# Prompt weight blocks nine beats apart, compressed rows turned later, and GpSimd signalling the end of a ranking stage

## Time and profile before

| what | value |
|---|---|
| three runs | 2637.49 us median (2624.43 to 2644.32) |
| the profiled execution | 2624.34 us, span 2622.6 us |
| granted TensorE clock, mean of the span | 0.857 |
| busy share of the span | PE 75%, DVE 56%, POOL 53%, PEld 38%, ACT 28% |
| moved by DMA | 806.19 MB, mean 307 GB/s |
| packets of GpSimd's queue (the expert rows and cached pages) | 68.1% of the time of 16 engines |
| packets of SP's queue (weights, stored rows) | 14.1% |

### The profile page before, as it was taken

The page is one execution under the profiler, slowest core; times in us unless marked ns, Lnnn a source line. Parts: engine busy times, 40 slices in busy tenths (PEclk is TensorE's granted clock), DMA queues, the critical chain, the costliest instruction groups (busy, mean ns, idle before and its releaser), DMA issues. The chain is left out here.

```text
span 2622.6 us, 23237 instructions
## 1 busy us (share of the span) xinstructions
PE 1959.6 (75%) x7254; PEld 1008.9 (38%) x7254; DVE 1462.1 (56%) x3293; ACT 721.4 (28%) x1716; POOL 1389.9 (53%) x1415
## 2 busy tenths in 40 slices
PE   5979798688988767986857889676677777748346
PEld 4446467244444324545412345352122323227111
DVE  1024346576465623674954268666366777763864
ACT  1111112366675402431211135111132333310001
POOL 2021016667677734674774356658465555443774
PEclk9975699798999887897979889788898999965579
DMA  7141509887999998899889989997989999896797
GB/s 222 65 160 44 177 1 335 311 306 283 383 408 411 406 385 294 325 351 403 321 326 400 307 328 347 386 335 255 390 335 360 358 358 372 296 349 232 275 392 305
DMA packets 253891, 806.19 MB, mean 307 GB/s; under 512 B 41813, under 2 KB 46425, under 8 KB 244249
## 3 DMA queue, kind: packets, MB, share of 16 engines
q0 software_dynamic: 176496, 673.82, 68.1%
q1 hardware_dynamic: 77128, 130.89, 14.1%
q10 hardware_dynamic: 144, 0.00, 0.0%
HBM read 798.90 MB, written 14.04 MB: 310 GB/s over the span
## 5 line engine op out<-in xcount | busy, mean ns | idle before, releaser
L3142 PE MATMUL g_acc<-g_vrow,g_diag 128*128 128x512 f32 (+1 forms) x1432 | 766.3, 670 | 260.2 <-ACT g_diag L3120 128.5
L3013 POOL DMA_INDIRECT g_vrow<-in_peer_v_dram,f_idx x576 | 598.2, 1039 | 458.1 <-PE g_acc L3142 161.6
L2997 POOL DMA_INDIRECT f_u<-in_peer_u_dram,f_idx x576 | 579.1, 1005 | 375.3 <-DVE g_dot L3078 244.3
L3078 DVE CUSTOM_DVE_ANT_0 f_u<-f_u,g_h_ps 128x1024 f32<-128x1024 f32 x576 | 685.1, 1214 | 116.8 <-DMA f_u<-in_peer_u_dram,f_idx 66.2
L3142 PEld LDWEIGHTS g_acc<-g_vrow,g_diag 128*128 128x128 f32 (+1 forms) x1432 | 262.9, 198 | 659.4 <-issue 460.4
L3055 DVE SCALAR_TENSOR_TENSOR x<-g_vrow,g_w,x 128x1024 f32<-128x1024 f32 x218 | 280.6, 1287 | 22.1 <-DMA g_vrow<-in_peer_v_dram,f_idx 11.6
L1068 ACT ACTIVATE g_slab<-g_side 64x256 f32<-64x256 f32 x512 | 193.8, 378 | 116.9 <-PE g_side L1019 110.8
L3039 DVE TENSOR_TENSOR g_w<-g_gelu,f_gate 128x4 f32<-128x4 f32 x144 | 26.3, 183 | 357.3 <-ACT g_gelu L3110 356.8
L1030 PE MATMUL g_side<-g_slab 128*128 128x512 f32 x256 | 144.2, 646 | 50.1 <-ACT g_slab L1068 50.0
L3120 ACT ACTIVATE g_diag<-const,g_w 128x128 f32<-128x128 f32 (+1 forms) x358 | 126.0, 381 | 195.8 <-DVE g_w L3039 194.4
L1170 PE MATMUL g_side<-g_slab 128*128 128x512 f32 (+3 forms) x288 | 129.6, 593 | 60.2 <-DMA g_slab<-in_nsa_w_in_dram 60.2
(11 more groups left out here) (402 smaller groups left out, 2407.8 us busy)
## 6 DMA issues: line engine op xcount, KB each, us to landing
g_slab<-in_nsa_w_in_dram SPq DMA_DIRECT2D x15, 2048.0 KB, 18.9
g_slab<-in_peer_w_q_dram SPq DMA_DIRECT2D x14, 2048.0 KB, 19.8
mp_w<-in_mlstm_w_in_dram SPq DMA_DIRECT2D x6, 2048.0 KB, 10.6
g_slab<-in_nsa_w_out_dram SPq DMA_DIRECT2D x6, 2048.0 KB, 14.4
f_u<-in_peer_u_dram,f_idx POOLq DMA_INDIRECT x576, 7.5
g_vrow<-in_peer_v_dram,f_idx POOLq DMA_INDIRECT x576, 7.5
g_slab<-in_state_win_kv_dram SPq DMA_DIRECT2D x8, 1024.0 KB, 8.9
out_win_s_dram<-in_state_win_kv_dram SPq DMA_DIRECT2D x1, 8128.0 KB
```

The costliest lines, as they stand in the source:

```text
L2997: pool.indirect_dma_start(u[:, i % RU, :], None, u_table, bass.IndirectOffsetOnAxis(ap=idx[:, col:col + 1], axis=0), element_offset=layer ...
L3013: pool.indirect_dma_start(vrow[:, i % RV, :], None, v_table, bass.IndirectOffsetOnAxis(ap=idx[:, col:col + 1], axis=0), element_offset=lay ...
L3078: dve.tensor_tensor_reduce(row, row, h_ps[:], 1.0, 0.0, ALU.mult, ALU.add, dot[:, g % 2, k:k + 1]).then_inc(dotted, 1)
L3142: mm = pe.matmul(acc[0:n, a, :], diag[:, q % (2 * GRP), 0:n], vrow[:, i % RV, a * 512:a * 512 + 512], start=first and on_pe[i] == on_pe[GR ...
```

## The change

- `NP_AT` has a row for prompts and one for the decode work. In the prompt stages the jobs begin at beats 0, 9, 18, 27, 29 and 38 of the projection instead of 0, 6, 12, 18, 20 and 26; their lengths stay. Steps that stood at fixed beats behind the jobs (adding the gate's bias, rotating and turning the queries) are now counted from the jobs. In the decode work the beats are as they were.
- `CMP` is 61 instead of 49, which is the same distance behind job 5. The second half of the compressed rows is turned nine beats (`NEXT_ROWS`) behind the first instead of four, and all that follows is five beats later.
- In a route stage VectorE no longer waits for `placed`; GpSimd adds the third 1 to `fence` right behind its last `place`.
- Ten beats instead of four lie between a route stage and what comes next.

So tile 0's route stage begins at beat 468 instead of 451, tile 1's prompt stage at 585 instead of 562 and its route stage at 769 instead of 729, and the decode work at 854 instead of 812. `SHARES`, `DENSE` and the slots are as they were.

```diff
-NP_AT = [0, 6, 12, 18, 20, 26]
+NP_AT = [[0, 9, 18, 27, 29, 38], [0, 6, 12, 18, 20, 26]]
 NP_LEN = [6, 6, 6, 2, 6, 6]
...
     def pe(self, pe, at, beat, t):            # Projection
-                yield from at(w0 + NP_AT[j] + NP_LEN[j] * c // DC)
+                yield from at(w0 + NP_AT[s][j] + NP_LEN[j] * c // DC)
...
-            yield from at(w0 + 38 + a)
+            yield from at(w0 + NP_AT[s][5] + 12 + a)
             self.turn(pe, t, a)
...
-    CMP = 49
-    ATT = CMP + 14
+    CMP = 61
+    NEXT_ROWS = 9
+    ATT = CMP + 10 + NEXT_ROWS
...
     def compress_pe(self, pe, at, beat, t):
         for e in range(2):
-            yield from at(beat + 4 * e)
+            yield from at(beat + self.NEXT_ROWS * e)
...
     def dve(self, dve, at, step, beat, t):    # RouteWork
         for m, (first, r, col, chunk) in enumerate(self.passes(beat, t)):
             yield from self.ranks.dve(dve, at, first, r, 4, 2 * NJ + 1 + NJ * t + 2 * m + 2, col, self.ranks.sc, chunk)
-        yield from at(beat + self.length(t))
-        S.leave(dve, self.ranks.placed, LAYER0_RANKS + 2 * t + 2)

     def pool(self, pool, at, beat, t):
         for first, r, col, chunk in self.passes(beat, t):
             yield from self.ranks.place(pool, at, first, r, 4, col, chunk)
+        self.S.leave(pool, self.ranks.placed, LAYER0_RANKS + 2 * t + 2)
...
-            beat = self.beats[t][1] + self.route.length(t) + 4
+            beat = self.beats[t][1] + self.route.length(t) + 10
```

More of the change, by code:

```diff
@@ L1199, in act @@
         for j, (_, cols) in enumerate(NP_JOBS):
-            yield from at(w0 + NP_AT[j] + NP_LEN[j] + 1)
+            yield from at(w0 + NP_AT[s][j] + NP_LEN[j] + 1)
             if j == 5:
@@ L1217, in act @@
         for a in range(2):
-            yield from at(w0 + 39 + a)
+            yield from at(w0 + NP_AT[s][5] + 13 + a)
             self.copy(act, t, a)
@@ L1255, in dve @@
         for br in range(3):
-            yield from at(w0 + NP_AT[br] + NP_LEN[br] + 3)
+            yield from at(w0 + NP_AT[s][br] + NP_LEN[br] + 3)
             dve.wait_ge(self.stored, 6 * t + br + 1)
             self.rotate(dve, step, t, kvh[0:n, br, 0])
-        yield from at(w0 + 23)
+        yield from at(w0 + NP_AT[s][3] + 5)
         dve.wait_ge(self.stored, 6 * t + 4)
@@ L1262, in dve @@
         dve.tensor_tensor(self.gate[0:n], self.gate[0:n], self.b_gate[0:n], ALU.add).then_inc(self.biased, 1)
-        yield from at(w0 + 35)
+        yield from at(w0 + NP_AT[s][5] + 9)
         dve.wait_ge(self.stored, 6 * t + 6)
@@ L1369, in compress_pe @@
             mm.then_inc(self.turned, 1)
-        yield from at(beat + 6)
+        yield from at(beat + self.NEXT_ROWS + 2)
         pe.wait_ge(self.copied_a, 2 * t + 2)
@@ L1381, in compress_pe @@
         mm.then_inc(self.multiplied, 1)
-        yield from at(beat + 11)
+        yield from at(beat + self.NEXT_ROWS + 7)
         pe.wait_ge(self.hid_ready, 2 * t + 2)
@@ L1539, in compress_act @@
         for e in range(2):
-            yield from at(beat + 4 * e + 1)
+            yield from at(beat + self.NEXT_ROWS * e + 1)
             self.copy_sub(act, t, e, 0)
-        yield from at(beat + 7)
+        yield from at(beat + self.NEXT_ROWS + 3)
         act.wait_ge(self.multiplied, t + 1)
@@ L1545, in compress_act @@
                        ).then_inc(self.second_ready, 1)
-        yield from at(beat + 9)
+        yield from at(beat + self.NEXT_ROWS + 5)
         act.wait_ge(self.pre_ready, t + 1)
@@ L1551, in compress_act @@
                            bias=self.b1[:, c:c + 1]).then_inc(self.hid_ready, 1)
-        yield from at(beat + 12)
+        yield from at(beat + self.NEXT_ROWS + 8)
         act.wait_ge(self.out_mm, t + 1)
@@ L1560, in compress_dve @@
         for e in range(2):
-            yield from at(beat + 4 * e + 1)
+            yield from at(beat + self.NEXT_ROWS * e + 1)
             self.copy_sub(dve, t, e, 1)
-        yield from at(beat + 8)
+        yield from at(beat + self.NEXT_ROWS + 4)
         dve.wait_ge(self.second_ready, t + 1)
```

## The result

The changed kernel takes 2667.45 us (median; 2661.83 to 2670.36) beside 2634.53 for the kernel before (2624.43 to 2644.32): ratio **1.0112** [1.0083, 1.0141], some 30 us slower. The forecast was 2632 us, with a range of 2600 to 2662 and a chance of 0.13 for slower. The profiled execution took 2669.13 us, its span 2667.3.

A forecast was written before the change was run, and what follows sets the result against it. DMA was taken as busy in most slices, so terms priced stretches where it was not. A to G: -12 - 4 + 0 + 10 + 3 + 1 - 3 = -5 us, 2632 on the median; range 2600 to 2662.

The forecast's parts named there:

- A: Weight blocks nine beats apart in the prompt projections: less backlog behind them, 12 us gained, ends 0 and 19.9.
- B: Compressed rows nine beats apart: shorter wait for the second half, 4 us gained; ends 11.6 gained, 6.2 lost.
- C: GpSimd signals the route stage's end: VectorE's waits go, 0 us taken; ends 14.1 gained, 3.7 lost.
- D: Fixed `SHARES` puts folds over later rankings and decode's blocks, loading VectorE: 10 us lost, ends 0 and 19.
- F: Matmuls instead of folds beside tile 1's output projection and tile 0's route stage: 1 us lost, ends 0 and 8.
- folds decide: Slower rival: VectorE bounds wherever D, E and F place work, costing 33.6 us; 2668 us, chance 0.13.
- third term: Part of D: more folded slots in decode's later blocks behind beat 918, 9.4 us, covered by VectorE's idle time.
- E: Tile 1's ranking covers fewer slots in dense beats, beside a busy VectorE: 3 us lost, 6.6 at most.
- losing end of 6.2: B's worst case: tile 1's weight loads take as long as tile 0's and leave a stall, 6.2 us lost.
- The losing mechanism: Under B: busy fetches slow the branch's small weight loads, as a projection without stalls keeps fetches flowing then.
- G: Decode work ends 42 beats later, leaving fewer slots in the tail: 3 us gained, 4.6 at most.

The follow-up runs named there:

- e11: Kernel before with stages as late as the changed kernel's, bounds of `SHARES` moved along, decode work at beat 848: 2624.41 us, ratio 0.9946.
- e9: Changed kernel with bounds of `SHARES` moved along and the decode work at beat 848 instead of 854: 2633.92 us, ratio 0.9986.
- e1: Changed kernel with the bounds of `SHARES` moved to where its stages now lie: 2642.55 us, ratio 1.0021.
- e18: Kernel before with stages as late as the changed kernel's and only one bound of `SHARES` moved, 742 to 782: 2651.37 us, ratio 1.0054.
- e4: Changed kernel with the weight blocks six beats apart again, the stages' beats held: 2678.83 us, ratio 1.0150.
- e17: e15 with the weight blocks nine beats apart alone, stages starting twelve beats earlier: 2626.63 us, ratio 0.9965.
- e15: Kernel before with late stages, bounds of `SHARES` moved along, decode work at beat 860: 2621.83 us, ratio 0.9930.
- e12: e5 with the compressed rows nine beats apart instead of four, stages starting five beats earlier: 2665.33 us, ratio 1.0095.
- e5: Kernel before with stages as late as the changed kernel's and bounds of `SHARES` moved along, decode at 854: 2634.90 us, ratio 0.9997.
- e6: Changed kernel with VectorE signalling the end of a ranking stage again instead of GpSimd: 2670.98 us, ratio 1.0117.

## Why the prediction was wrong

The 1.12% can be walked from the kernel before to the changed one by kernels in between:

| step | from, to | change of the ratio |
|---|---|---|
| late stages, bounds along, decode at 848 | before, e11 | -0.54% |
| blocks, rows and signal | e11, e9 | +0.40% |
| decode from 848 to 854 | e9, e1 | +0.35% |
| bounds as they were | e1, after | +0.91% |

Two steps of the sum failed, and a third was not in it. A, B and C were to return 16 us and together cost 10.5: 26 us of the miss, by the account of A and B. D and F were to cost 11 and cost 24: 13 us, above all by the size of F. The decode work's beat was no step at all: it cost 9 (the intervals of e9 and e1 just overlap), against 14 gained by the later stages, which the sum had at nothing. That is 26 + 13 - 5 = 34, from a forecast of 5 gained to a loss of some 30.

**D and F, the bounds that stayed: sized 11, measured 24.** The rival "folds decide" had the time, 2668, by luck: it had it by VectorE, which was not what decided. The working failed in F: "DMA is mostly full there: 1 lost". I counted 5.3 us of matmuls and looked at DMA in the slots where they fall. The count was too low: each of the two matmuls of a slot stands in the trace as two records (1432 for 358 unfolded slots), and by the page's 766.3 us an unfolded slot costs TensorE 2.14 us, not 1.18, so 9.6 us for tile 1 and 4.8 for tile 0. And TensorE's own later work, the projection for the ranking, is what they delayed, by 5 us of time and 9 of TensorE beside a ranking pass. e18 gives the bound at 742 6 to 9 us. D's 10 was the two rankings, 4.8 each, with the third term (9.4) held to be covered by idle time; it came out the other way. VectorE was full in the rankings, as forecast, but the second pass of tile 1 took 36 us in the changed kernel and 34 in e1, with the bounds moved. The third term cost some 6 us, in the first nine slots of the parts, not in the blocks themselves, where DMA stayed at 411 GB/s. These places are read from one profiled execution each, and 9 to 12 of the 24 us are not placed. E was not tried by itself; it is in the first row of the table.

**A, blocks: its own place right, its sum wrong.** One long wait at job 4 and over 300 GB/s behind it, as forecast, and 10 us in e4, near the 12 (the intervals overlap). The waits for blocks hardly shrank, 43.5 us in both tiles instead of 45.0: in tile 0 a load now took a median of 21.4 us, instead of 18.9. But I stopped the account at the end of the projection. The backlog that A removes was what made DMA slack for the small loads behind; with it gone they wait (e17 against e15, which differ in the spacing and in the stages' first beat alone). Alone the spacing returns nothing and probably loses (e17). This is the step that I would do otherwise: A and B were priced as separate stretches, and A's gain in the one is paid for in the other.

**B, rows: wrong sign.** Forecast 4 gained, one wait of 11 us in tile 0; measured waits of 21.7 and 22.7 us, one in each tile, and alone a loss of 26 (e12), beyond the losing end of 6.2. The losing mechanism that I wrote down was the one that ran: the same four loads land after 5.1 us beside low fetches (e5) and after 19.3 beside more of them (e12). The rule of the Trainium skill (DMA: Bandwidth & Descriptors, Queues, rings and completion order) that DMA engines take their queues in turn spoke for it, and the trace agrees as far as it shows. The losses of A and B don't add: with the blocks nine apart, the loads are slow and the rows late whether the rows stand four or nine apart (42.7 us of waits in e17, 44.3 in the changed kernel), and all three edits together cost 10.5 us (e9 against e11).

**C, signal: right, as far as can be told.** 0 forecast, -0.05% between e6 and the changed kernel, with intervals of 11 and 8 us to either side. The waits came back at the entry, as forecast. Over the whole run the 218 folds took 280.4 us, before 280.6, and GpSimd's ranking products (L1861, before L1860) 43.7 us, before 44.5. So the 7.7 us that the Trainium skill's rule on VectorE and GpSimd (SBUF — State Buffer, Who interferes with whom) would have made of it do not show.

**G, and what I did not see.** Late stages with everything moved along are *faster* by 0.54% (e11) to 0.70% (e15), where E and G together came to nothing in my sum. The waits for the stored rows are part of it: 7.1 us in e15. Why the small loads meet a slacker DMA at beats 370 and 651 than at 353 and 611 is not settled. And no term of mine asked how the decode work stands to the folded slots; the 42 beats by which it moved are six modulo twelve, and that cost 9 us (e1 against e9; 13 in e5 against e11).

## What to carry to other kernels

When a stall is removed, ask what used the slack that it left: here the small loads behind tile 1's projection landed after 5.2 us while it was blocked (e15), and after 25.6 us with the blocks nine apart (e17). A table that is written in absolute positions belongs to the work that it was balanced for, and moves with it. Where a repeated piece of work and a repeated pattern of slots have a common period, move the work by whole periods, or try each place: eight beats alone were worth 21 us, and moving all stages by 17 to 48 beats with both rules kept made this kernel 0.70% faster [0.47, 0.92].

## What the runs showed of the hardware

Four loads of 256 KB from one queue landed after a median of 5.1 us (e5, tile 1) or of 25.6 to 27.4 us (the changed kernel), the later the more fetches ran beside them. And 41 us of VectorE's waits at the end of a stage could be exchanged for 25 us at the entry of the next with a change of 0.05% in the time, within intervals of 0.3 to 0.4% to either side.
